# Two transformer blocks in one kernel: phase borders worked in column halves, a five-slab weight ring with the low parts in place, and loops written out

## The chip, the cores and the metric

The kernel runs on one core of a Trainium2 chip. A core has a matrix engine (TensorE, PE in the profile; its weight loads are PEld), a vector engine (VectorE, DVE), an activation engine (ScalarE, ACT), GpSimd (POOL) and a queue engine (SyncE, SP) that here issues most of the transfers. All work from SBUF, the on-chip memory of 128 partitions; PE writes to PSUM. The metric is the device time of one execution in microseconds, as the median of several.

## The reference

A 256 x 1024 activation goes through four layers' worth of sublayers in fp32. Cut to what matters:

```
h = x
h += gating_mixer(rms_norm(h)); h += relu(rms_norm(h) @ w_up[0])**2 @ w_down[0]          # "gate_in/gate_out", "mlp0"
h += dilated_attention(rms_norm(h)); h += relu(rms_norm(h) @ w_up[1])**2 @ w_down[1]     # "qkv/attn/attn_out", "mlp1"
x = rms_norm(h) * final_norm_g                                                            # "final1"
for i in range(2):
    shift, scale, gate = (silu(c) @ ada_w[i] + ada_b[i]) split in three for each of 3 sublayers
    x += 0.5 * gate0 * swiglu(rms_norm(x) * (1 + scale0) + shift0, ffn_w_in, ffn_w_out)   # "ffn0", "ffn2"
    x += gate1 * (pool_mixer if i == 0 else conv_mixer)(... )                             # "pool", "conv_in/conv_out"
    x += 0.5 * gate2 * swiglu(rms_norm(x) * (1 + scale2) + shift2, ...)                   # "ffn1", "ffn3"
return rms_norm(x) * final_g
```

d_model is 1024, the hidden width of an mlp 4096, that of an ffn 2816. The weights are some 340 MB and each is used once.

## The kernel before

**Phases and slabs.** The names at the right above are the phases, run one after the other. Tokens lie in two blocks of 128 (t = 0, 1). Weights come in *slabs* of 128 x 2048 fp32 (1 MB, two transfers each): an mlp chunk has four (two of w_up, two of w_down), 8 chunks; an ffn chunk has three (two of w_in, one of w_out), 11 chunks; 245 slabs in all. A slab is used as two fp32r parts: ACT copies `raw` to `w_hi` (L512), DVE subtracts to get `w_lo` (L865). A product is then three matmuls per tile: w_hi with xT_hi, w_lo with xT_hi, w_hi with xT_lo (L1315). `xT_hi/xT_lo` hold the normed activation transposed, `hT_hi/hT_lo` the hidden one; `up_ps` and `acc` are the PSUM results of the up and down product, `tr_ps` takes transposes (L1396).

**Ring.** `raw`, `w_hi` and `w_lo` have three places each (RING). SP loads slab n when n - 3 has been split by ACT and DVE; ACT and DVE split n when PE has used n - 3. `ahead(g)` stands in ACT's and DVE's order about where PE works on slab g, and splits slab g + 3.

**Steady chunk.** PE does the up product of chunk c (48 matmuls), then the down product of chunk c - 1, then transposes chunk c's hidden tile (`mid`). ACT and DVE make `mid` from up_ps in between, and DVE also accumulates the conditioning product `ada_acc` (L930, L933) from transfers of 1 MB that ACT issues (in mlp0, mlp1, part of qkv, ffn0, ffn1).

**A border.** The order is written out by hand on each engine and joined by semaphores. PE finishes `acc` for block 0 (`acc0_ready`), then block 1 (`slab_used`). DVE (`enter`, L900) does `products(0)`: the gated product (L968, in the second model block) and the residual addition (L971), 1024 columns each; ACT squares and sums the row (L534); POOL makes 1/rms in two steps (L476, L470); DVE scales to `xn` (L880); PE transposes xn (`turn_norm`, eight transposes); ACT applies the norm's gain (L547, L549); DVE splits into xT_hi and xT_lo (L886, L887). `first_chunk` on PE turns block 0 of the *next* phase after the last matmul of the old one, does slab g for block 0, turns block 1, and does slab g + 1 for block 0, then both slabs for block 1. In `enter` one w_lo split stands ahead of block 1's xT splits and one at the end (`before`, `after`). At mlp1 to ffn0, `final1` and the ffn's own norm follow each other (L1139 between).

The long phases' middle chunks are loops on every engine (`Fori`; three chunks a body in an mlp, one in an ffn).

## Time and profile before

| | |
|---|---|
| median of 3 runs | 1605.37 us (1604.02 to 1610.68) |
| the profiled execution | 1607.08 us, its span 1605.3 us |
| PE busy | 1524.8 us, 95% |
| PE weight loads | 1254.0 us, 78% |
| DVE busy | 1038.2 us, 65% |
| ACT busy | 707.9 us, 44% |
| read from HBM | 343.96 MB, 215 GB/s over the span |
| mean granted TensorE clock | 0.981 |

Matmuls overlap in the records (one of 512 columns is shown with about 0.4 us), so a rate is read from the distance of starts. Idle time of an engine is given in brackets with what ended it.

### The profile page before, as it was taken

Reading aid. Unit: us, or ns where it says so; the run is one execution under the profiler, and the core shown is the slowest. Engines: PE = TensorE matmul, PEld = TensorE weight load, DVE = VectorE, ACT = ScalarE, POOL = GpSimd, SP = SyncE. Lnnn points to the kernel's source line nnn. Section 1 sums busy time; section 2 is a strip of 40 time slices with the busy share of each in tenths; the row PEclk is TensorE's granted clock in tenths of the full one; section 3 lists DMA queues with packets and bytes.
Section 4 is the critical chain, followed back from the end, with each engine's and each line's share of the span. In section 5 each row is a group of like instructions: output and inputs, shape, how many; then the busy total and the mean of one; then the engine's idle time right before and its main releaser. Section 6 shows DMA issues by size and latency. Waiting matters only on the chain.

```text
span 1605.3 us, 20507 instructions
## 1 busy us (share of the span) xinstructions
PE 1524.8 (95%) x7069; PEld 1254.0 (78%) x7069; DVE 1038.2 (65%) x1110; ACT 707.9 (44%) x831; POOL 22.0 (1%) x63
## 2 busy tenths in 40 slices
PE   5899999999999999799998899998999999999997
PEld 4778888788778888678887788886788878778886
DVE  4748777545548767567887778887645464764444
ACT  5345444543545454444443434444344444454442
POOL 1000000000000000000000000000000000000000
PEclk9999999999999999899999899999999999999999
DMA  8438777557508788558896279886455546445552
GB/s 260 174 126 324 270 269 274 159 173 243 175 12 295 282 287 289 188 183 309 302 311 229 85 256 318 303 313 217 144 184 188 189 140 204 143 158 185 190 190 76
DMA packets 201892, 345.83 MB, mean 215 GB/s; under 512 B 9531, under 2 KB 105027, under 8 KB 201836
## 3 DMA queue, kind: packets, MB, share of 16 engines
q1 hardware_dynamic: 161420, 267.22, 49.5%
q10 hardware_dynamic: 40416, 77.86, 13.9%
q8 instruction: 35, 0.57, 0.1%
q14 instruction: 21, 0.17, 0.0%
HBM read 343.96 MB, written 1.09 MB: 215 GB/s over the span
## 4 chain that ended last, share of the span: by engine, by line
PE 84%; DVE 8%; ACT 3%; DMA 2%; issue 2%; POOL 1%; SPq 0%; POOLq 0%; DVEq 0%; ACTq 0%
PE up_ps L1315 51%; PE acc L1315 28%; DVE w_lo L865 3%; PE tr_ps L1396 2%; DMA ada_raw<-in_ada_w 2%; PE tr_ps L1315 1%; DVE ada_acc L933 1%; ACT w_hi L512 1%; DVE res L971 1%; ACT xn L534 1%; DVE xn L968 1%; PE tr_ps L1581 1%; ACT xn L549 1%; PE tr_ps L1495 1%; POOL rstd L470 1%
## 5 line engine op out<-in xcount | busy, mean ns | idle before, releaser
L865 DVE TENSOR_TENSOR w_lo<-raw,w_hi 128x2048 fp32r<-128x2048 f32 x245 | 561.1, 2291 | 302.4 <-ACT w_hi L512 301.3
L512 ACT ACTIVATE w_hi<-raw 128x2048 fp32r<-128x2048 f32 x245 | 469.5, 1916 | 313.1 <-PE up_ps L1315 256.7
L1315 PE MATMUL up_ps<-w_hi,xT_hi 128*128 128x512 f32 x1264 | 506.0, 400 | 22.8 <-DVE xT_lo L887 16.5
L1315 PE MATMUL up_ps<-w_hi,xT_lo 128*128 128x512 f32 x1264 | 497.5, 394 | 0.0
L1315 PE MATMUL up_ps<-w_lo,xT_hi 128*128 128x512 f32 x1264 | 497.1, 393 | 0.0
L1315 PEld LDWEIGHTS up_ps<-w_hi,xT_hi 128*128 128x128 f32 x1264 | 240.4, 190 | 75.3 <-issue 16.9
L1315 PEld LDWEIGHTS up_ps<-w_hi,xT_lo 128*128 128x128 f32 x1264 | 240.1, 190 | 51.4
L1315 PEld LDWEIGHTS up_ps<-w_lo,xT_hi 128*128 128x128 f32 x1264 | 240.8, 190 | 47.6
L933 DVE SCALAR_TENSOR_TENSOR ada_acc<-ada_raw,cond,ada_acc 128x512 f32 (+1 forms) x252 | 189.3, 751 | 15.7 <-DMA ada_raw<-in_ada_w 8.0
L1315 PE MATMUL acc<-w_hi,hT_hi 128*128 128x512 f32 x624 | 194.3, 393 | 4.8 <-DVE hT_lo L876 4.8
L1315 PE MATMUL acc<-w_hi,hT_lo 128*128 128x512 f32 x624 | 193.0, 391 | 0.0
L1315 PE MATMUL acc<-w_lo,hT_hi 128*128 128x512 f32 x624 | 192.9, 391 | 0.0
L1315 PEld LDWEIGHTS acc<-w_hi,hT_hi 128*128 128x128 f32 x624 | 116.5, 188 | 30.1 <-DVE hT_lo L876 4.0
L526 ACT ACTIVATE hT_hi<-tr_ps 128x256 fp32r<-128x256 f32 (+1 forms) x122 | 47.8, 441 | 207.4 <-PE tr_ps L1396 203.6
L1315 PEld LDWEIGHTS acc<-w_lo,hT_hi 128*128 128x128 f32 x624 | 117.7, 189 | 24.6
L1315 PEld LDWEIGHTS acc<-w_hi,hT_lo 128*128 128x128 f32 x624 | 117.5, 188 | 24.5
L876 DVE TENSOR_TENSOR hT_lo<-tr_ps,hT_hi 128x256 fp32r<-128x256 f32 (+1 forms) x122 | 55.4, 494 | 75.7 <-ACT hT_hi L526 75.4
L752 ACT ACTIVATE pre<-up_ps 128x256 f32<-128x256 f32 x88 | 33.9, 385 | 134.4 <-PE up_ps L1315 134.3
L534 ACT ACTIVATE xn<-res 128x1024 f32<-128x1024 f32 x24 | 25.7, 1072 | 78.6 <-DVE res L971 70.0
L1167 DVE TENSOR_TENSOR mid<-pre,up_ps 128x256 f32<-128x256 f32 x88 | 34.9, 416 | 22.8 <-ACT pre L752 22.8
L1396 PE MATMUL tr_ps<-flip,xn 128*128 128x128 f32 x160 | 26.4, 318 | 20.1 <-DVE xn L880 15.9
L1396 PEld LDWEIGHTS tr_ps<-flip,mid 128*128 128x128 f32 x304 | 36.6, 140 | 11.2 <-issue 4.2
(121 smaller groups left out, 788.6 us busy)
## 6 DMA issues: line engine op xcount, KB each, us to landing
raw<-in_ffn_w_in SPq DMA_DIRECT2D x176, 512.0 KB, 4.7
ada_raw<-in_ada_w ACTq DMA_DIRECT2D x72, 1024.0 KB, 6.9
raw<-in_ffn_w_out SPq DMA_DIRECT2D x88, 512.0 KB, 4.4
raw<-in_w_up SPq DMA_DIRECT2D x64, 512.0 KB, 4.7
raw<-in_w_down SPq DMA_DIRECT2D x64, 512.0 KB, 4.6
raw<-in_b_w_qkv SPq DMA_DIRECT2D x36, 512.0 KB, 4.4
raw<-in_conv_w_in SPq DMA_DIRECT2D x24, 512.0 KB, 4.6
raw<-in_a_w_in SPq DMA_DIRECT2D x16, 512.0 KB, 6.3
```

Source lines behind the costliest of these rows:

```text
L470: nc.gpsimd.tensor_tensor(dst, src, neg_half[:, 0:1], ALU.pow).then_inc(ready, 1)
L512: nc.scalar.activation(w_hi[:, slot, :], raw[:, slot, :], ACT.Copy).then_inc(hi_ready, 1)
L526: nc.scalar.activation(dst, src, ACT.Copy).then_inc(tr_hi, 1)
L534: nc.scalar.activation(xn[:, t, :], res[:, t, :], ACT.Square, accum_out=sumsq[:, t:t + 1]).then_inc(sumsq_ready[t], 1)
L549: a = nc.scalar.activation(dst, src, ACT.Identity, bias=bias, scale=scale)
L752: nc.scalar.activation(pre[:, t, 0:HALF], up_ps[:, t, 0:HALF], ACT.Silu).then_inc(silu_done, 1)
L865: nc.vector.tensor_tensor(w_lo[:, slot, :], raw[:, slot, :], w_hi[:, slot, :].bitcast(F32), ALU.subtract).then_inc(lo_ready, 1)
L876: nc.vector.tensor_tensor(lo, src, hi.bitcast(F32), ALU.subtract).then_inc(tr_read, 1)
L933: a = nc.vector.scalar_tensor_tensor(out=dst, in0=src, scalar=cond[:, k:k + 1], in1=dst, op0=ALU.mult, op1=ALU.add)
L1167: nc.vector.tensor_tensor(mid[:, t, 0:HALF], pre[:, t, 0:HALF], up_ps[:, t, HALF:UPN], ALU.mult).then_inc(ffn_mid, 1)
L1315: return nc.tensor.matmul(dst, a, b, start=start, stop=stop, skip_group_check=True)
L1396: last = nc.tensor.transpose(dst[:, q * P:(q + 1) * P], tile, ident)
```

## The change

- The ring has five places. `w_lo` is placed at the address of `raw`: DVE writes the low part over the slab it came from. SP may therefore load slab n only when PE has used slab n - 5; ACT and DVE no longer wait for PE themselves. `ahead(g)` splits slab g + 4.
- At the end of a phase PE makes `acc` in column halves of 512 (`down_halves`), each with a signal of its own (`acc_ready`), and the transposes of the next phase's block 0 stand between the two halves of block 1 (not at mlp1 to ffn0, where they stand behind, nor at the pool).
- Products, additions, squares and the scaling of a border are done in halves; the two partial sums are added by POOL's first step. xT is split in pairs of 128-column tiles, each waited for by PE. Block 1's transposes come two k-tiles later in PE's order. DVE's order in `enter` is another.
- The tails of mlp and ffn are reordered: the transposes of the last hidden chunk come earlier. In an ffn's last chunk DVE makes `mid` ahead of its w_lo split.
- The output is stored in four pieces. All `Fori` loops are written out. Some small tiles lie elsewhere (`o_tok` in xT_hi, `bias_t` in hT).

```diff
...
-RING = 3
+RING = 5
+LEAD = RING - 1
...
+        raw_at = -(-nc.sbuf_base // 32) * 32
         raw = sb("raw", [P, RING, SLAB])
+        w_lo = nc.alloc_sbuf_tensor_at("w_lo", [P, RING, SLAB], F32R, offset=raw_at)
...
             def load(g, src, view):
...
+                slot = g % RING
+                if g >= RING:
+                    sp.wait_ge(slab_used, g - RING + 1)
...
+            def split_hi(n):
+                if n < N_SLABS:
+                    slot = n % RING
                     act.wait_ge(raw_landed[slot], 32 * (n // RING + 1))
...
+                    nc.scalar.activation(w_hi[:, slot, :], raw[:, slot, :], ACT.Copy).then_inc(hi_ready, 1)
+            def ahead(g):
+                split_hi(g + LEAD)
...
+            def squares(n, t):
+                for c in range(2):
+                    if n:
+                        act.wait_ge(res_ready[t], 2 * n + c - 1)
...
+                    cols = slice(c * COLS, (c + 1) * COLS)
+                    nc.scalar.activation(xn[:, t, cols], res[:, t, cols], ACT.Square, scale=D ** -0.5,
+                                         accum_out=sumsq[:, t, c:c + 1]).then_inc(sumsq_ready[t], 1)
...
             def scale_tokens(n, t):
                 dve.wait_ge(rstd_ready[t], n + 1)
-                nc.vector.tensor_scalar(xn[:, t, :], res[:, t, :], rstd[:, t:t + 1], None, ALU.mult)\
-                    .then_inc(xn_ready, 1)
...
+                for c in range(2):
+                    cols = slice(c * COLS, (c + 1) * COLS)
+                    nc.vector.tensor_scalar(xn[:, t, cols], res[:, t, cols], rstd[:, t:t + 1], None, ALU.mult)\
+                        .then_inc(xn_ready, 1)
...
+            def norm_split(name, t, ks=range(0, KT, 2)):
+                for k in ks:
+                    fill = (KT // FILL) * t + k // FILL
+                    if k % FILL == 0:
+                        dve.wait_ge(y_half, NORM_FILLS * XT[name] + fill + 1)
+                    else:
+                        dve.wait_ge(tr_read, at[name].tr + fill + 1)
...
+                    own(nc.vector.tensor_copy(hi, src))
+                    nc.vector.tensor_tensor(lo, src, hi.bitcast(F32), ALU.subtract).then_inc(xT_ready, 1)
...
             def enter(name, products, before=(), after=(), last_norm=None):
-                products(0)
+                for c in range(2):
+                    products(0, c)
+                for g in before:
+                    ahead(g)
                 if last_norm is not None:
                     last_norm(0)
+                    for c in range(2):
+                        products(1, c)
                 scale_tokens(NORM[name], 0)
-                products(1)
+                if last_norm is None:
+                    products(1, 0)
                 if name in XT:
-                    norm_split(name, 0)
-                if last_norm is not None:
+                    norm_split(name, 0, (0, 2))
+                if last_norm is None:
+                    products(1, 1)
+                else:
                     last_norm(1)
+                if name in XT:
+                    norm_split(name, 0, (4, 6))
                 scale_tokens(NORM[name], 1)
-                for g in before:
-                    ahead(g)
                 if name in XT:
                     norm_split(name, 1)
                 for g in after:
                     ahead(g)
...
+                def products(t, c):
+                    if sub is not None and (t, c) == (0, 0):
                         dve.wait_ge(gate_ready, sub + 1)
-                    if t == 0:
-                        dve.wait_ge(acc0_ready, product + 1)
+                    if (t, c) == (TT - 1, 1):
+                        dve.wait_ge(slab_used, g + 1)
                     else:
-                        dve.wait_ge(slab_used, g + 1)
-                    src = acc[:, t, :]
+                        dve.wait_ge(acc_ready, 3 * product + 2 * t + c + 1)
+                    cols = slice(c * COLS, (c + 1) * COLS)
+                    src = acc[:, t, cols]
                     if gate is not None:
-                        own(nc.vector.scalar_tensor_tensor(out=xn[:, t, :], in0=src, scalar=gate,
-                                                           in1=gate_B[:, sub % 3, :], op0=ALU.mult, op1=ALU.mult))
-                        src = xn[:, t, :]
-                    nc.vector.tensor_tensor(res[:, t, :], res[:, t, :], src, ALU.add).then_inc(res_ready[t], 1)
+                        own(nc.vector.scalar_tensor_tensor(out=xn[:, t, cols], in0=src, scalar=gate,
+                                                           in1=gate_B[:, sub % 3, cols], op0=ALU.mult, op1=ALU.mult))
+                        src = xn[:, t, cols]
+                    nc.vector.tensor_tensor(res[:, t, cols], res[:, t, cols], src, ALU.add).then_inc(res_ready[t], 1)
...
+                def step(c, g):
                     if c == 1:
                         for m in MODS.get(name, ())[:1]:
                             modulation(name, m)
-                    ahead(g, i, 3)
+                    at_end = c == FFN_CHUNKS - 1
+                    if not at_end:
+                        ahead(g)
                     if unit0 is not None and c >= 2:
-                        ada(unit0 + c - 2, 0, i, 1)
-                    gated_mid(c, i)
-                    ahead(g + 1, i, 3)
+                        ada(unit0 + c - 2, 0)
+                    for t in range(TT):
+                        gated_mid(c, t)
+                    ahead(g if at_end else g + 1)
                     if c == 1:
                         for m in MODS.get(name, ())[1:]:
                             modulation(name, m)
...
+                    if at_end:
+                        transposed(c, 2)
+                        return
+                    transposed(c)
                     if unit0 is not None and c >= 2:
-                        ada(unit0 + c - 2, 1, i, 1)
...
+                        ada(unit0 + c - 2, 1)
+                    ahead(g + 2)
...
-            enter("pool", residual(last("pool"), 4, 0.5, 0), [last("pool") - 1])
+            enter("pool", residual(last("pool"), 4, 0.5, 0), [last("pool") - 2, last("pool") - 1])
...
-            enter("ffn2", residual(last("ffn2"), 6, 0.5, 2), [last("ffn2") - 1], [last("ffn2")])
+            enter("ffn2", residual(last("ffn2"), 6, 0.5, 2), [last("ffn2") - 2], [last("ffn2") - 1, last("ffn2")])
...
+                for q in qs:
                     k = s * UPK + q
+                    if x0 is not None and k % 2 == 0:
+                        pe.wait_ge(xT_ready, x0 + KT // 2 * t + k // 2 + 1)
...
+            def down_halves(g, t, hi, lo, k0, between=None):
+                for c in range(2):
+                    if c and between is not None:
+                        between()
+                    last = down_tile(g, t, hi, lo, k0, False, (c,), True)
+                    if (t, c) != (TT - 1, 1):
+                        last.then_inc(acc_ready, 1)
+                return last
...
+            def down_last(g, hi, lo, k0, start, ready=None, between=None):
+                for t in range(TT):
+                    if ready is not None:
+                        pe.wait_ge(tr_read, ready[0] + (t + 1) * ready[1])
                     if t == 0:
-                        last.then_inc(acc0_ready, 1)
...
+                        pe.wait_ge(lo_ready, g + 1)
+                    last = down_tile(g, t, hi, lo, k0, start)
+                    if t == 1:
+                        last.then_inc(slab_used, 1)
+                    else:
+                        pe.wait_ge(lo_ready, g + 2)
+                    last = down_halves(g + 1, t, hi, lo, k0 + 2, between if t else None)
+                last.then_inc(slab_used, 1)
...
             def turn_norm(name, t):
-                pe.wait_ge(xn_ready, 2 * XN[name] + t + 1)
-                if t == 0:
-                    pe.wait_ge(tr_read, at[name].tr)
                 for b in range(KT // FILL):
+                    pe.wait_ge(xn_ready, 4 * XN[name] + 2 * t + b + 1)
+                    if (t, b) == (0, 0):
+                        pe.wait_ge(tr_read, at[name].tr)
                     turn(xn, t, b * FILL, FILL, at[name].tr + (KT // FILL) * t + b)
...
+            def first_chunk(name, turned=True):
                 g = at[name].slab
...
+                x0 = TT * KT // 2 * XT[name]
+                if not turned:
+                    turn_norm(name, 0)
+                pe.wait_ge(lo_ready, g + 1)
+                up_tile(g, 0, 0, x0=x0)
+                pe.wait_ge(lo_ready, g + 2)
+                up_tile(g + 1, 1, 0, range(0, 2), x0)
+                turn_norm(name, 1)
+                up_tile(g + 1, 1, 0, range(2, UPK), x0).then_inc(up0_ready, 1)
+                up_tile(g, 0, 1, x0=x0).then_inc(slab_used, 1)
+                up_tile(g + 1, 1, 1, x0=x0).then_inc(slab_used, 1)
...
+                c = MLP_CHUNKS - 1
+                gb = g + 4 * c - 2
+                up_chunk(gb, (relu_done, 2 * (m0 + c - 1) + 1))
+                down_slab(gb + 2, hT_hi, hT_lo, 0, False, (mid_fill(p, name, c - 1), 1))
+                pe.wait_ge(lo_ready, gb + 4)
+                down_tile(gb + 3, 0, hT_hi, hT_lo, 2, False)
+                turn_mid(c, 0)
+                down_tile(gb + 3, 1, hT_hi, hT_lo, 2, False).then_inc(slab_used, 1)
+                turn_mid(c, 1)
+                down_last(gb + 4, hT_hi, hT_lo, 0, False, (mid_fill(p, name, c), 1),
+                          (lambda: turn_norm(after, 0)) if early else None)
+                if not early:
+                    turn_norm(after, 0)
...
                 c = FFN_CHUNKS - 1
                 gb = g + 3 * c - 1
-                up_chunk(gb, free=(ffn_mid, 2 * (f0 + c - 1) + 1, 0))
+                up_chunk(gb, (ffn_mid, 2 * (f0 + c - 1) + 1))
                 ready = mid_fill(p, name, c - 1)
+                turn_mid(c, 0)
                 pe.wait_ge(lo_ready, gb + 3)
-                pe.wait_ge(tr_read, ready + 2)
-                down_tile(gb + 2, 0, hT_hi, hT_lo, 0, False, False)
-                turn_mid(c)
-                down_tile(gb + 2, 1, hT_hi, hT_lo, 0, False, False, [0])
+                down_tile(gb + 2, 0, hT_hi, hT_lo, 0, False)
+                turn_mid(c, 1)
                 pe.wait_ge(lo_ready, gb + 4)
                 pe.wait_ge(tr_read, ready + 3)
-                down_tile(gb + 3, 0, hT_hi, hT_lo, 2, False, True).then_inc(acc0_ready, 1)
-                down_tile(gb + 2, 1, hT_hi, hT_lo, 0, False, False, [1]).then_inc(slab_used, 1)
+                down_halves(gb + 3, 0, hT_hi, hT_lo, 2)
+                down_tile(gb + 2, 1, hT_hi, hT_lo, 0, False).then_inc(slab_used, 1)
                 pe.wait_ge(tr_read, ready + 4)
-                down_tile(gb + 3, 1, hT_hi, hT_lo, 2, False, True).then_inc(slab_used, 1)
...
+                down_halves(gb + 3, 1, hT_hi, hT_lo, 2,
+                            (lambda: turn_norm(after, 0)) if after in XT else None).then_inc(slab_used, 1)
...
```

DVE at the border ffn1 to ffn2, before, from the last silu product on (L865 w_lo split, L880 scaling, L886 and L887 the split of xn):

```order
L1167 TENSOR_TENSOR mid<-pre,up_ps 128x256 [waits silu_done] x2
L865 TENSOR_TENSOR w_lo<-raw,w_hi 128x2048 [waits slab_used,hi_ready]
L876 TENSOR_TENSOR hT_lo<-tr_ps,hT_hi 128x2x128 [waits tr_hi] x2
L968 SCALAR_TENSOR_TENSOR xn<-acc,region 128x1024 [waits acc0_ready,gate_ready]
L971 TENSOR_TENSOR res<-res,xn 128x1024 [waits dve_step]
L880 TENSOR_SCALAR xn<-res,rstd 128x1024 [waits rstd_ready0]
L968 SCALAR_TENSOR_TENSOR xn<-acc,region 128x1024 [waits slab_used]
L971 TENSOR_TENSOR res<-res,xn 128x1024 [waits dve_step]
L886 CAST xT_hi<-xn 128x2x128 [waits y_half]
L887 TENSOR_TENSOR xT_lo<-xn,xT_hi 128x2x128 [waits dve_step]
L886 CAST xT_hi<-xn 128x2x128 [waits tr_read]
```

After (L831 w_lo split, L847 scaling, L940 and L943 product and addition, L860 and L861 the split of xn):

```order
L940 SCALAR_TENSOR_TENSOR xn<-acc,region 128x512 [waits acc_ready,gate_ready]
L943 TENSOR_TENSOR res<-res,xn 128x512 [waits dve_step]
L940 SCALAR_TENSOR_TENSOR xn<-acc,region 128x512 [waits acc_ready]
L943 TENSOR_TENSOR res<-res,xn 128x512 [waits dve_step]
L831 TENSOR_TENSOR w_lo<-raw,w_hi 128x2048 [waits hi_ready]
L847 TENSOR_SCALAR xn<-res,rstd 128x512 [waits rstd_ready0]
L847 TENSOR_SCALAR xn<-res,rstd 128x512
L940 SCALAR_TENSOR_TENSOR xn<-acc,region 128x512 [waits acc_ready]
L943 TENSOR_TENSOR res<-res,xn 128x512 [waits dve_step]
L860 CAST xT_hi<-xn 128x2x128 [waits y_half]
L861 TENSOR_TENSOR xT_lo<-xn,xT_hi 128x2x128 [waits dve_step]
L860 CAST xT_hi<-xn 128x2x128 [waits tr_read]
```

The 1024-column steps have become pairs of 512, the w_lo split stands ahead of the scaling, and block 1's first half is added ahead of the first xT pair.

PE at the border gate_out to mlp0, before: the last three matmul pairs of block 1, the transposes of xn, the first matmuls of mlp0.

```order
L1315 MATMUL acc<-w_hi,xT_hi 128x512 x2
L1315 MATMUL acc<-w_lo,xT_hi 128x512 x2
L1315 MATMUL acc<-w_hi,xT_lo 128x512 x2
L1396 MATMUL tr_ps<-flip,xn 128x128 [waits tr_read,xn_ready]
L1396 MATMUL tr_ps<-flip,xn 128x128 x3
L1396 MATMUL tr_ps<-flip,xn 128x128 [waits tr_read]
L1396 MATMUL tr_ps<-flip,xn 128x128 x3
L1315 MATMUL up_ps<-w_hi,xT_hi 128x512 [waits xT_ready,lo_ready]
L1315 MATMUL up_ps<-w_lo,xT_hi 128x512
L1315 MATMUL up_ps<-w_hi,xT_lo 128x512
```

After, from the same place, with the transposes between the halves of block 1:

```order
L1284 MATMUL acc<-w_hi,xT_hi 128x512
L1284 MATMUL acc<-w_lo,xT_hi 128x512
L1284 MATMUL acc<-w_hi,xT_lo 128x512
L1376 MATMUL tr_ps<-flip,xn 128x128 [waits tr_read,xn_ready]
L1376 MATMUL tr_ps<-flip,xn 128x128 x3
L1376 MATMUL tr_ps<-flip,xn 128x128 [waits tr_read,xn_ready]
L1376 MATMUL tr_ps<-flip,xn 128x128 x3
L1284 MATMUL acc<-w_hi,xT_hi 128x512
L1284 MATMUL acc<-w_lo,xT_hi 128x512
L1284 MATMUL acc<-w_hi,xT_lo 128x512
L1284 MATMUL acc<-w_hi,xT_hi 128x512
L1284 MATMUL acc<-w_lo,xT_hi 128x512
```

Six matmuls into acc now stand behind the transposes of xn and ahead of the first up product.

## Rows read from the trace of the kernel before

**Rows 1.** Stretches: us; PE, PEld, DVE, ACT, POOL busy; granted clock, DMA share, GB/s.

```profile
800.00:840.00 40.00, 40.00 (x183) 33.11 (x182) 32.75 (x37) 16.41 (x18) 0.00 (x0) 1.00 0.90 307
```

**Rows 2.** Timeline of PE, mlp0: start, duration, operation; transposes that end chunks.

```profile
189.20 1.03 PE L1396 MATMUL tr_ps<-flip,mid 128*128 128x128 f32 x8
...
211.85 1.04 PE L1396 MATMUL tr_ps<-flip,mid 128*128 128x128 f32 x8
...
234.53 1.03 PE L1396 MATMUL tr_ps<-flip,mid 128*128 128x128 f32 x8
```

**Rows 3.** Waits of PE: total us, times, longest us.

```profile
PE up_ps L1315 <- DVE xT_lo L887: 16.5, 9, 4.1
PE tr_ps L1396 <- DVE xn L880: 15.9, 10, 3.6
...
PE acc L1315 <- DVE hT_lo L876: 4.8, 6, 1.9
```

**Rows 4.** Timeline of PE, ffn1 to ffn2; in brackets idle before and releaser.

```profile
1090.17 0.70 PE L1315 MATMUL acc<-w_hi,hT_hi 128*128 128x512 f32 x2 [0.48 <-DVE hT_lo L876]
...
1098.69 1.09 PE L1396 MATMUL tr_ps<-flip,xn 128*128 128x128 f32 x8 [1.45 <-DVE xn L880]
...
1101.84 0.76 PE L1315 MATMUL up_ps<-w_hi,xT_hi 128*128 128x512 f32 x1 [2.06 <-DVE xT_lo L887]
...
1107.33 0.50 PE L1315 MATMUL up_ps<-w_hi,xT_hi 128*128 128x512 f32 x1 [0.24 <-DVE w_lo L865]
```

**Rows 5.** Timeline of DVE and ACT, same border, chain of block 0.

```profile
1093.27 1.23 DVE L968 SCALAR_TENSOR_TENSOR xn<-acc,region 128x1024 f32<-128x1024 f32 x1 [2.92 <-PE acc L1315]
...
1094.53 1.23 DVE L971 TENSOR_TENSOR res<-res,xn 128x1024 f32<-128x1024 f32 x1
...
1095.79 1.06 ACT L534 ACTIVATE xn<-res 128x1024 f32<-128x1024 f32 x1 [7.01 <-DVE res L971]
...
1097.88 0.75 DVE L880 TENSOR_SCALAR xn<-res,rstd 128x1024 f32<-128x1024 f32 x1 [2.13 <-POOL rstd L470]
```

**Rows 6.** Groups by form, DVE and ACT: busy us, mean ns, then idle.

```profile
L865 DVE TENSOR_TENSOR w_lo<-raw,w_hi 128x2048 fp32r<-128x2048 f32 x245 | 561.1, 2291 | 302.4 <-ACT w_hi L512 301.3 <-DVE region L1247 0.9
...
L876 DVE TENSOR_TENSOR hT_lo<-tr_ps,hT_hi 128x512 fp32r<-128x512 f32 x34 | 22.0, 686 | 16.9 <-ACT hT_hi L526 16.9
...
L930 DVE TENSOR_SCALAR ada_acc<-ada_raw,cond 128x512 f32 x28 | 13.5, 481 | 0.0
...
L512 ACT ACTIVATE w_hi<-raw 128x2048 fp32r<-128x2048 f32 x245 | 469.5, 1916 | 313.1 <-PE up_ps L1315 256.7 <-PE acc L1315 51.7 <-DMA raw<-in_a_w_in 2.9
...
L628 ACT ACTIVATE pre<-up_ps 128x512 f32<-128x512 f32 x32 | 19.2, 599 | 35.1 <-PE up_ps L1315 35.1
```

**Rows 7.** Timeline of PE, mlp0 to qkv.

```profile
295.14 0.47 PE L1315 MATMUL up_ps<-w_hi,xT_hi 128*128 128x512 f32 x1 [1.19 <-DVE xT_lo L887]
...
298.51 1.09 PE L1396 MATMUL tr_ps<-flip,xn 128*128 128x128 f32 x8 [0.37 <-DVE xn L880]
...
300.71 0.50 PE L1315 MATMUL up_ps<-w_hi,xT_hi 128*128 128x512 f32 x1 [1.11 <-DVE w_lo L865]
```

**Rows 8.** Timeline of PE, mlp1 to ffn0.

```profile
654.06 1.08 PE L1315 MATMUL acc<-w_hi,hT_hi 128*128 128x512 f32 x2 [1.86 <-DVE hT_lo L876]
...
669.09 1.09 PE L1396 MATMUL tr_ps<-flip,xn 128*128 128x128 f32 x8 [2.23 <-DVE xn L880]
...
671.58 0.77 PE L1315 MATMUL up_ps<-w_hi,xT_hi 128*128 128x512 f32 x1 [1.40 <-DVE xT_lo L887]
...
679.01 1.33 PE L1396 MATMUL tr_ps<-flip,xn 128*128 128x128 f32 x5 [2.97 <-DVE xn L880]
```

**Rows 9.** Timeline of PE, the pool's first matmuls.

```profile
881.04 8.15 PE L1315 MATMUL tr_ps<-region,xn 128*128 128x128 f32 x48 [4.05 <-DVE xn L880]
```

**Rows 10.** Timeline of PE, second chunk of gate_in.

```profile
33.46 0.47 PE L1315 MATMUL up_ps<-w_hi,xT_hi 128*128 128x512 f32 x1 [1.35 <-ACT region L606]
```

**Rows 11.** Loads of raw issued inside ffn0: us from issue to landing.

```profile
DMA to landing us min/median/max: 3.9/5.7/7.6
```

594 lines of the change are left out of this document (243 added, 351 removed).

## Prediction

> **What bounds the kernel now.** I read the page's busy times first: TensorE (PE) is busy 95% of the span. Then the table by stretches: inside the big layers PE is busy all of 40 us, at the full granted clock, even where the DMA share is 0.90 [rows 1]. The timeline of PE gives the rate there: an mlp0 chunk of 96 matmuls of 512 columns and 8 transposes takes 22.65 us [rows 2]; with 0.8 for the transposes that is 0.228 us a matmul, and 5.5 us for a slab of 24. So the layers themselves give nothing. What is left is what PE waits for: about 80 us, and the longest entries in the list of waits are the norm's split output xT_lo (16.5 us in 9 waits), the norm's scaled output xn (15.9 us in 10) and hT_lo (4.8 us) [rows 3]. All of them lie at the border between one phase and the next.
>
> **One border, read closely (ffn1 to ffn2).** PE waits 0.48 us for hT_lo, 1.45 for xn, 2.06 for xT_lo, and then runs at the lower clock: from 1101.84 to 1107.33 us lie 12 matmuls and 8 transposes, nominally 12 x 0.228 + 0.6 = 3.3 us, and the waits inside are 0.24, so 1.9 us go to the clock; the first matmul takes 0.76 us against 0.50 in the later row, so the granted clock has fallen to its 1.2 GHz level after 3.5 us of waits [rows 4]. The sum is 4.2 us of waits and 1.9 of clock. The chain that PE waits for is serial: gated product 1.23, addition 1.23, square 1.06 (and about 0.2 to read its sum), two steps on GpSimd (they lie in the 2.13 us that DVE waits for rstd), scaling 0.75 [rows 5].
>
> **The change at such a border.** PE finishes token block 0 of acc by column halves. Call T0 the end of its second half. Before, 18 or 24 matmuls stand behind T0 ahead of the transposes (4.1 or 5.5 us); now always 18 (4.1 us), then transposes, then 6 matmuls (1.4 us) that cover the split of xn. Price of the pieces on DVE: 512-column operations with two inputs 0.69, scaling 0.48; on ACT 0.60 [rows 6], plus 0.2 for the sum. The gated pair I take as 0.75 + 0.69, a little over the nearest row. The first half is accumulated 1.4 us before T0, so its products run until T0 + 0.3, those of the second until T0 + 1.7; square T0 + 2.55, GpSimd T0 + 3.5. Here the changed DVE order has one w_lo split (2.29 [rows 6]) ahead of the scaling, which therefore ends its first half at T0 + 4.5: PE arrives at 4.1 and waits 0.4. First xT pair: DVE does the products of block 1's first half until 6.35, then the pair until 7.1; PE has its transposes and the 6 matmuls until 7.0, wait 0.2. The next pairs come at 7.8, 9.95 and 10.7 and PE needs them at 8.5, 9.9 and later; block 1's xn is there at 11.4 when PE comes at 11.3. The wait for hT_lo stays at about 0.5, since one w_lo split still stands ahead of it on DVE. Sum of waits about 1.25 instead of 4.2, no single one long, so I take the clock as staying up. Worth 3.0 + 1.9 = **5 us**, and the same at ffn2 to conv_in: **10 us** for the two.
>
> *What a rule makes of the pieces.* The row shows that a 1024-column operation takes 1.22 to 1.23 and a 512-column one 0.69, so each extra instruction costs 0.15 us [rows 5, 6]. The Trainium skill (Perfetto Trace Analysis, Optimizing Scalar/DVE Operations) gives an access overhead of some 60 ns on SBUF and 125 ns on PSUM for a DVE instruction; by that the two halves would be about 0.1 us cheaper per pair and each gated border 0.2 us better. The measured rows decide.
>
> **Ungated borders.** gate_out to mlp0, mlp0 to qkv, attn_out to mlp1 have the same shape without the gate and with no w_lo split inside the border (slabs are now split four ahead, so g+1 is ready: that was the 1.11 us in [rows 7]). There the scaled half is ready at T0 + 3.1, before PE's 4.1, and the first pair at about 6.2 to 6.6 against PE's 6.5: waits of 0 to 0.2. Their waits before are 1.19 + 0.37 + 1.11 = 2.7 [rows 7], and at mlp0 to qkv about 1 more for hT_lo (the rest of the six in [rows 3]). Worth 2.7, 3.6 and 2.7. conv_out to ffn3 is gated without a split and had 2.1 + 0.2 + 1.1: worth 3.3. Together **12 us**.
>
> **mlp1 to ffn0**, with two norms in a row, lies otherwise: 1.86 + 2.23 + 1.40 + 2.97 us of waits, and a lower clock after them [rows 8]. New chain for block 0: products T0 + 0.95, first norm T0 + 2.7, its two output halves 4.2, second square 5.0, GpSimd 5.9, then block 1's products, which are queued in front, 6.4, scaling 6.9; PE has nothing left at T0 + 5.5 and waits 1.4, then 1.1 for the first pair. The third pair is queued on DVE behind block 1's last norm (rstd at T0 + 12.9, two halves until 14.4): a wait of some 3.3 us where PE had none. Block 1's xn follows at 16.6 instead of 17.7, with 30 matmuls behind it where there were 36 (1.4 us). That is 2.5 us, or up to 3.8 if the clock is up. The hT_lo wait shrinks from 1.86 to about 0.8 by the split tail, and with it goes the low clock behind it (the first pair takes 1.08 us there and 0.70 in [rows 4]), 1.6 us by estimate from the 1.9 above. Taken: **5.5 us** (3 to 8).
>
> **The pool phase gives nothing back.** PE waits 4.05 us for xn there [rows 9] and needs both blocks whole. The changed DVE order has two w_lo splits (4.6 us) between block 0's products and its scaling, which at their end (T0 + 6.7) come 3 us behind rstd; the last tail ends its block 0 about 1 us earlier, the pieces cost 0.6. I get the start of the pool 1.2 us later and ffn1's border behind it 0.8 us better: **-0.4** (-2 to +2).
>
> **Start.** ACT now does four w_hi splits and the fifth ahead of the first gelu, one more than before, 1.92 us [rows 6], and PE transposes block 1 six matmuls later. PE already waits 1.35 us for that gelu [rows 10]; I work out 2.8: **-1.4** (-2 to 0).
>
> **End.** After the last matmul the last half has 0.75 + 0.69 in place of 1.23 + 1.23, square 0.8 in place of 1.25, but two output pieces in place of one: **+1.2**.
>
> **Loops written out: 0.** The transposes that end mlp0's chunks lie 22.65 us apart inside the old loop body of three and 22.68 across its branch [rows 2], so a branch costs PE 0.03 us at most; 40 such ends are 1 us. The Trainium skill (Runtime: NRT & Kernel Launch, Instruction fetch mechanics) says that a taken branch to code outside the resident pages must wait for a fetch, which would make written-out code faster; the interval does not agree, and the page alone has no price for it.
>
> **Loads: the cost that the change adds.** SP's load of slab n waited for the splits of n-3; now it waits until PE has used n-5 (the low part sits in raw's place). Behind it are queued later loads, ACT's w_hi split of n, and behind that ACT's silu and, on DVE, w_lo, the ada sums and mid. In ffn0 and ffn1, the tightest stages, a load lands 5.7 us (3.9 to 7.6) after issue [rows 11]. Released at a chunk's start and landed at +6.2, it gives w_hi at 8.1, w_lo at 10.4, ada until 13.2, mid at 14.0; PE asks for mid at 16.4 of its 16.8 us. So 2.4 us are spare, and 1 at the 7.6 us landing. Bounds: 0 by that, and at a landing of 11 us, which no row there has, 2.4 us per chunk. I take 0.
>
> **Sum:** 10 + 12.3 + 5.5 - 0.4 - 1.4 + 1.2 = 27 us. The profiled execution took 1607.1 (span 1605.3); the median of the three runs is 1605.4. 1605.4 - 27 = **1578**.
>
> **Rivals.** (a) Half the gain: DVE's own queue gives the time back, because the products of block 1 and the splits stand ahead of the xT pairs, and every piece that is 0.2 us dearer than taken shifts PE at eight borders. If waits of 1.5 us stay at each and the clock falls at the two gated ones, 6 x 1.2 + 4 = 11 to 14 us are lost: 1591. For it: the spare times above are a few tenths. (b) The other side: the later loads. Place: ffn0 and ffn1, 16 chunks with two ada loads each. It starts at landings over 8.6 us and makes the kernel slower than before by 0.5% where they reach 6.2 + 2.4 + (27 + 8)/16 = 10.8 us; at 11.5 it is 1605 - 27 + 46 = 1624. Against it: loads now come one by one instead of in bursts, and the longest there is 7.6 [rows 11]. (c) More than taken: clock up also through mlp1 to ffn0 and the pool, whose lower clock the stretch after them shows, and no start penalty: 27 + 9 = 36 us, 1569. (d) The change doesn't shorten the chain: signals for halves are there, but DVE is still held by an earlier entry of its queue (the w_lo split that needs a late w_hi), so xn comes when it came before: 1602 to 1608.
>
> **How the numbers follow.** Forecast (1573 to 1584) 0.52; (a) 0.22, (c) 0.12, (b) 0.07, (d) 0.07. The range that leaves out (b) and (d) and most of the tail of (a): 1567 to 1593. A run of this kernel can tell about 0.5%, 8 us: faster than 1597 0.87, within 0.05, slower 0.08.
>
> **What would show it.** Right: PE's waits for xT_lo and xn fall from 32 to under 12 us; the granted clock has no dip at ffn1 to ffn2 and ffn2 to conv_in but has one at mlp1 to ffn0 and the pool; PE's steady chunks stay 16.8 us; the wait for the first gelu grows to 2.8. Wrong: idle PE inside ffn0 or ffn1 chunks that ends with mid or w_lo (b), or waits of over 1 us for xT_lo at the gated borders (a).

## Result and profile after: 1596.6 us, a ratio of 0.9948

The changed kernel takes 1596.6 us (median of 5, 1594.7 to 1601.7) where the kernel before takes 1605.4; the ratio is 0.9948, 95% interval 0.9927 to 0.9969. Faster, as forecast, but by 9 us and not by 27, so the time lies above the range (1567 to 1593). Here and below, a ratio is taken between executions of both kernels in one session, and can differ by some 0.002 from the quotient of the two medians. The page of after, with the engines' busy time, the chain that ended last, and the group of ScalarE's (ACT's) splits:

```profile
span 1594.8 us, 17438 instructions
PE 1523.5 (96%) x7069; PEld 1249.8 (78%) x7069; DVE 1047.8 (66%) x1220; ACT 713.4 (45%) x879; POOL 32.9 (2%) x63
...
PE 80%; DVE 9%; DMA 4%; ACT 3%; issue 1%; POOL 1%; SPq 0%; DVEq 0%; POOLq 0%; ACTq 0%
...
L498 ACT ACTIVATE w_hi<-raw 128x2048 fp32r<-128x2048 f32 x245 | 469.1, 1918 | 287.8 <-DMA raw<-in_ffn_w_in 132.3
```

The last row is the first hint: the split of a slab now waits for its DMA. In the kernel before the same group waited for PE. The groups by line, first of before and then of after, show who ended the idle time ahead of the splits:

```profile
L512 ACT ACTIVATE w_hi<-raw 128x2048 fp32r<-128x2048 f32 x245 | 469.5, 1916 | 313.1 <-PE up_ps L1315 256.7 <-PE acc L1315 51.7 <-DMA raw<-in_a_w_in 2.9
...
L498 ACT ACTIVATE w_hi<-raw 128x2048 fp32r<-128x2048 f32 x245 | 469.1, 1918 | 287.8 <-DMA raw<-in_ffn_w_in 132.3 <-DMA raw<-in_w_up 42.0 <-DMA raw<-in_w_down 31.0
```

PE's waits of after (waited for: us in total, times, longest), against [rows 3]:

```profile
PE tr_ps L1376 <- DVE xn L847: 9.7, 6, 3.3
PE up_ps L1284 <- DVE xT_lo L861: 7.4, 4, 3.8
...
PE acc L1284 <- DVE hT_lo L841: 5.7, 5, 3.7
...
PE tr_ps L1465 <- DVE mod_sum L915: 4.0, 3, 2.5
PE acc L1284 <- ACT region L676: 3.9, 1, 3.9
PE up_ps L1284 <- DVE mid L1138: 3.6, 3, 1.2
```

The border waits have halved (xT_lo and xn from 32.4 to 17.1 us). In their place stand waits that the prediction did not have: 3.9 us of attention's first matmul for ACT's copies (0.8 in the kernel before), 4.0 for `mod_sum`, the sums of the conditioning that PE's next transposes need (1.7 before), 3.6 for mid, and one of 3.7 for hT_lo.

**Where the time went, step by step.** I took the start of each first matmul of a chunk from PE's timeline of both kernels and subtracted. Gains are positive:

```
stage                               predicted   measured
start and gate_in                     -1.4        -2.4
gate_out to mlp0                      +2.7        +3.0
mlp0 to qkv                           +3.6        +3.6
qkv's last chunk and attention         0          -5.3
attn_out to mlp1                      +2.7        +3.4
mlp1, second chunk                     0          -4.2
mlp1 to ffn0                          +5.5        +2.1
pool and its borders                  -0.4        +1.0
ffn1, second and third chunk           0          -2.1
ffn1 to ffn2                          +5          +2.6
ffn2 to conv_in                       +5          +4.6
conv_out to ffn3                      +3.3        +2.3
end                                   +1.2        +1.5
steady chunks and the rest             0          +0.4
sum                                   +27         +10.5 (spans 1605.3, 1594.8)
```

So the six plain borders brought 19.5 of the 22.3 us that were summed for them, and 11.6 us went in three stages where the prediction had written 0; 3.4 more went at mlp1 to ffn0. Two of the places, read closely.

**Attention.** ACT in after (start, duration, [idle before <- what ended it]); L676 are the copies out of qkv's last chunks that PE waits for:

```profile
389.24 1.92 ACT L498 ACTIVATE w_hi<-raw 128x2048 fp32r<-128x2048 f32 x1 [5.24 <-DMA raw<-in_b_w_out]
391.06 0.58 ACT L676 ACTIVATE region<-up_ps 128x512 f32<-128x512 f32 x1
...
398.55 1.92 ACT L498 ACTIVATE w_hi<-raw 128x2048 fp32r<-128x2048 f32 x1 [5.48 <-DMA raw<-in_b_w_out]
404.17 1.91 ACT L498 ACTIVATE w_hi<-raw 128x2048 fp32r<-128x2048 f32 x1 [3.70 <-DMA raw<-in_w_up]
405.99 1.06 ACT L676 ACTIVATE region<-up_ps 128x512 f32<-128x512 f32 x2
```

and what SyncE issued (start, duration of the issue), with PE's matmul behind:

```profile
382.52 1.36 SPq L302 DMA_DIRECT2D bias_t<-bias_rows  x2
387.03 0.83 SPq L331 DMA_DIRECT2D raw<-in_b_w_out  x2
```

```profile
407.20 1.12 PE L1284 MATMUL acc<-region 64*128 64x128 f32 x7 [3.88 <-ACT region L676]
```

The second slab of attn_out is asked for at 387.03 and its split starts at 398.55: 11.5 us. The next one comes late too, and both copies, whose sums PE had finished at about 401 and 403, stand behind its split. PE's first score matmul comes 14.9 us after the start of qkv's last chunk and not 11.8. So 3.1 of attention's 5.3 us are this wait; the other 2.2 are lost behind it, where PE's granted clock is lower (the rows are with a_move below).

**mlp1 to ffn0.** ACT, then PE:

```profile
652.64 1.91 ACT L498 ACTIVATE w_hi<-raw 128x2048 fp32r<-128x2048 f32 x1 [5.64 <-DMA raw<-in_ffn_w_in]
654.46 1.07 ACT L508 ACTIVATE hT_hi<-tr_ps 128x512 fp32r<-128x512 f32 x2
```

```profile
657.54 0.80 PE L1284 MATMUL acc<-w_hi,hT_hi 128*128 128x512 f32 x1 [3.74 <-DVE hT_lo L841]
```

The first hT tile was in PSUM from 650.6; ACT held it for 3.9 us behind a slab of the next phase. So 1.86 us of [rows 8] became 3.74, and the gain of the split border behind it (waits of 1.18, 1.40 and 1.17 us, where 1.4, 1.1 and 3.3 had been worked out) was eaten.

### The profile page after: what moved, and what is told of

Its sections match the earlier page's. It is cut to its first block, busy times and chain, and to the rows that moved or that the text cites. A ratio compares the mean times of both kernels' runs of the same rounds, so it can differ in the third digit from the quotient of the medians.

```text
span 1594.8 us, 17438 instructions
## 1 busy us (share of the span) xinstructions
PE 1523.5 (96%) x7069; PEld 1249.8 (78%) x7069; DVE 1047.8 (66%) x1220; ACT 713.4 (45%) x879; POOL 32.9 (2%) x63
## 4 chain that ended last, share of the span: by engine, by line
PE 80%; DVE 9%; DMA 4%; ACT 3%; issue 1%; POOL 1%; SPq 0%; DVEq 0%; POOLq 0%; ACTq 0%
PE up_ps L1284 48%; PE acc L1284 27%; PE tr_ps L1376 3%; DVE w_lo L831 3%; DMA raw<-in_ffn_w_in 2%; ACT w_hi L498 2%; PE tr_ps L1284 1%; DVE ada_acc L904 1%; DMA raw<-in_w_down 1%; DVE res L943 1%; DVE xn L940 1%; DMA raw<-in_w_up 1%; PE tr_ps L1558 1%; ACT xn L518 1%; DVE xT_lo L861 1%
## 5 line engine op out<-in xcount | busy, mean ns | idle before, releaser
L831 DVE TENSOR_TENSOR w_lo<-raw,w_hi 128x2048 fp32r<-128x2048 f32 x245 | 559.3, 2289 | 289.9 <-ACT w_hi L498 289.7
L1284 PE MATMUL acc<-w_hi,hT_hi 128*128 128x512 f32 x624 | 199.9, 394 | 5.7 <-DVE hT_lo L841 5.7
L1284 PE MATMUL acc<-w_hi,hT_lo 128*128 128x512 f32 x624 | 197.9, 391 | 0.0
L1284 PE MATMUL acc<-w_lo,hT_hi 128*128 128x512 f32 x624 | 197.7, 391 | 0.0
L904 DVE SCALAR_TENSOR_TENSOR ada_acc<-ada_raw,cond,ada_acc 128x512 f32<-128x512 f32 x252 | 189.1, 751 | 12.8 <-DMA ada_raw<-in_ada_w 5.1
L841 DVE TENSOR_TENSOR hT_lo<-tr_ps,hT_hi 128x256 fp32r<-128x256 f32 (+1 forms) x122 | 55.7, 492 | 46.0 <-ACT hT_hi L508 45.5
L518 ACT ACTIVATE xn<-res 128x512 f32<-128x512 f32 x48 | 30.6, 638 | 56.7 <-DVE res L943 48.6
L1376 PE MATMUL tr_ps<-flip,mid 128*128 128x128 f32 x304 | 44.5, 273 | 2.7 <-DVE mid L1138 1.4
```

Of the source, the lines that this page charges most:

```text
L518: nc.scalar.activation(xn[:, t, cols], res[:, t, cols], ACT.Square, scale=D ** -0.5, accum_out=sumsq[:, t, c:c + 1]).then_inc(sumsq_ready[ ...
L831: nc.vector.tensor_tensor(w_lo[:, slot, :], raw[:, slot, :], w_hi[:, slot, :].bitcast(F32), ALU.subtract).then_inc(lo_ready, 1)
L841: nc.vector.tensor_tensor(lo, src, hi.bitcast(F32), ALU.subtract).then_inc(tr_read, 1)
L904: a = nc.vector.scalar_tensor_tensor(out=dst, in0=src, scalar=cond[:, k:k + 1], in1=dst, op0=ALU.mult, op1=ALU.add)
L1284: return nc.tensor.matmul(dst, a, b, start=start, stop=stop, skip_group_check=True)
L1376: last = nc.tensor.transpose(dst[:, q * P:(q + 1) * P], tile, ident)
```

## The experiments

**Theory L (late loads).** In the kernel before, the load of slab n is released by the splits of n-3, and its own split stands three slabs of PE time later in ACT's order. In the changed kernel it is released when PE has used n-5 and its split stands four slabs ahead of use: one slab, 5.5 us, lies between. A load with company takes longer, and everything behind the split in ACT's order waits. **Theory D (order)**: ACT and DVE now split four slabs ahead (a *lead* of four), which puts one more low part (2.29 us) ahead of urgent work on VectorE (DVE). **Rival R**: the halves bring less than summed, the ring costs nothing.

### Parts alone: b_flat, b_ring5, a_ring3, a_lead3

b_flat is the kernel before with its loops written out:

```
-                with pe.Fori(0, MLP_BODIES) as i:
-                    for b in range(MLP_BODY):
-                        step(2 + b, False, i, MLP_BODY)
+                for c in range(2, MLP_CHUNKS):
+                    step(c, False)
```

> The kernel before with its loops written out and nothing else: same instructions, same order, same ring of three. All theories: no effect of its own, 1605.4 +/- 1.5 us. If it is off by more than 3 us, part of the missing gain belongs to the written-out loops (the larger program), not to the ring.

Measured: ratio 0.999 (0.9978 to 1.0003), 1606.6 us. Written-out loops do nothing, as predicted. A trace is of one execution, and b_flat's shows how far to trust a single stage: with the same work in the same order as before, it is 0.9 us shorter at mlp1 to ffn0, 1.2 at the pool and its borders, and 0.5 longer in attention.

b_ring5 adds the ring to b_flat, the borders stay whole:

```
-RING = 3
+RING = 5
+LEAD = RING - 1
...
-                        sp.wait_ge(hi_ready, n - RING + 1)
-                        sp.wait_ge(lo_ready, n - RING + 1)
+                        sp.wait_ge(slab_used, n - RING + 1)
...
-                n = g + RING
+                n = g + LEAD
```

> The kernel before (borders whole, tails in the old order, loops written out) with only the ring changed: five slabs, low parts in place, a load released by the use of the slab five before, splits four slabs ahead. Theory L (late loads: a load now starts only when PE has used slab n-5, and its split stands in ScalarE's order one slab's use later, about 5.6 us, while landings with company take 4 to 10 us; the late split holds what stands behind it): the ring alone costs what the phases of the changed kernel show against the kernel before away from the borders, 3.9 (attention) + 4.2 (mlp1, second chunk) + 2.6 (gate_in) + 2.1 (ffn1) = 12.8 us and something at the borders: 1618 us, 1612 to 1624. Rival R (the borders in halves simply bring less than summed, the ring is free): 1605 +/- 2.

Measured: 1622.1 us, ratio 1.0085 (1.0063 to 1.0107). The ring alone costs 14 us; its trace has the loss at attention (8.1 us), in mlp1's second chunk (2.7), in and ahead of ffn1 (5.3) and at ffn1 to ffn2 (2.6), and 5 to 6 us of gain at the other borders, where the second slab is ready earlier. R falls, at least for the ring.

a_ring3 is the changed kernel with the old ring, a_lead3 the changed kernel with `LEAD = RING - 2`. Both need the low part of a phase's second slab placed by hand in DVE's order at seven borders:

```
                 scale_tokens(NORM[name], 1)
+                for g in second:      # last(name) - 1
+                    ahead(g)
                 if name in XT:
                     norm_split(name, 1)
```

> The changed kernel with the ring of before (three slabs, low parts in a buffer of their own, a load released by the split of the slab three before), borders in halves, reordered tails and written-out loops kept. Theory L: the 18 us that are missing come back for the most part: 1580 us, 1577 to 1586; before attention PE no longer waits 3.9 us, mlp1's second chunk takes 26.6 us and not 30.8. Rival R: the halves bring only what was measured, 1596 +/- 3.

> The changed kernel with its ring of five in place, but each slab split three slabs ahead of its use instead of four, so that one slab's use more (about 5.6 us) lies between the release of a load and its split. Theory L: most of the waits <-DMA raw of ScalarE and the waits behind them go: 1585 us, 1579 to 1589. Rival R: 1596 +/- 3. Rival C (the loads are late for lack of DMA throughput, not for their late start): little changes either, 1593 to 1598, and a_ring3 likewise stays high.

Measured: 1621.0 us (1.0072, 1.0050 to 1.0093) and 1620.1 us (1.0068, 1.0048 to 1.0089). Both missed, by 41 and 35 us, but not for the reason that was asked after. The stages in question did as L says: mlp1's second chunk took 27.0 us in a_ring3 and 25.8 in a_lead3 (30.8 in after), ffn1's chunks lost nothing, and from mlp1's last chunk to ffn0's first matmul a_lead3 needed 4.8 us less than the kernel before. But PE had a new wait (a_ring3):

```profile
PE up_ps L1288 <- DVE w_lo L834: 29.5, 7, 7.2
```

Seven waits, one for each border: with halves, PE arrives at the second slab before DVE has scaled the second block and come to its low part. In this placement it takes the lead of four to have the second slab ready in time.

### The second slab earlier, and late splits moved away: a_ring3b, a_lead3b, a_move, a_lead3bm

a_ring3b and a_lead3b move the two added lines above `scale_tokens`.

> a_ring3 with one instruction of VectorE moved at seven borders: the low part of a phase's second slab is made before the second tile is scaled, not behind it. In a_ring3 PE stood 29.5 us in seven waits for that low part. Theory L with this placement as the reason that a_ring3 came out slow: the seven waits go and the borders return to the changed kernel's own steps (first chunks 2 us shorter than before, where a_ring3 has them 3.1 to 4.7 longer), 38 us less than a_ring3: 1583 us where the kernel before is 1608, 1578 to 1590, so under the changed kernel. Rival P (the old ring can't give the second slab early, since its split waits for PE's use of the last slabs of the phase ahead): the waits move but stay, 1600 to 1615.

> a_lead3 with the same instruction moved. Theory L: 1582 us where the kernel before is 1608, 1577 to 1589: attention starts without the 3.9 us wait of the changed kernel, mlp1's second chunk takes 26 and not 30.8 us, mlp1 to ffn0 gets its 5 us. Rival P: the waits for the second slab's low part stay at half or more, 1600 to 1612.

Measured: 1599.3 us (0.9950, 0.9933 to 0.9968) and 1597.3 us (0.9940, 0.9920 to 0.9959), 16 and 15 us over what was expected. Some 22 us came back of the 38; the wait is still there (a_ring3b):

```profile
PE up_ps L1288 <- DVE w_lo L834: 16.5, 7, 4.0
```

So rival P was half right. The halves with the old ring give 0.9950, with the new ring 0.9948: the same total from different places. The changed kernel buys the second slab in time at seven borders, and pays for it in attention, mlp1, gate_in and ffn1.

a_move leaves ring and lead alone and only moves splits behind urgent copies (the same on DVE); three of its places:

```
                 hidden(0, 1, g)
-                ahead(g + 1)
                 transposed(0)
+                ahead(g + 1)
...
                     ahead(g + 1)
+                    if c == MLP_CHUNKS - 1:
+                        transposed(c)
                     ahead(g + 2)
-                    transposed(c)
+                    if c < MLP_CHUNKS - 1:
+                        transposed(c)
...
-                if u == 1:
-                    ahead(at["attn"].slab - 1)
+                if u in (1, 4):
+                    ahead(at["attn"].slab - (2 if u == 1 else 1))
```

> The changed kernel, ring of five and lead of four as they are; only the order on ScalarE and VectorE changes at four places, so that no split of a late slab stands ahead of work that PE waits for: in qkv's last chunk and in attention (one split moved behind the copies), and in both mlps' first and last chunk (one split moved behind the copies of the turned hidden values). Theory L (the harm is done by what stands behind a late split, in order): 3.9 us at attention, 4.2 in mlp1's second chunk, 3.4 of mlp1 to ffn0 come back, 1587 us, 1583 to 1592, and nothing changes in the ffns. Rival S (PE itself waits for late slabs and would wait for them anyway): 1596 +/- 2.

Measured: 1592.5 us (0.9908, 0.9890 to 0.9925), 4 us under the changed kernel by the medians and 6 by the ratios (1587 was expected). By stages: mlp1 to ffn0 got its 3.7 us back, as expected. In mlp1's second chunk only 0.7 of 4.2 came back: the order of ACT's splits is not the reason there. In attention PE's first score came at 11.8 us again, the 3.1 us of waiting were gone, and yet the stage ended only 0.2 us earlier, because what followed ran at a lower granted clock. Stretches of 10 us (busy PE, PEld, DVE, ACT, POOL, then the granted clock, DMA share, GB/s), first before, then after, then a_move, then b_ring5_ada4 of further down:

```profile
405.00:415.00 10.00, 7.28 (x34) 5.63 (x32) 7.77 (x10) 5.28 (x8) 0.00 (x0) 0.85 0.74 248
415.00:425.00 10.00, 9.95 (x57) 8.23 (x56) 5.37 (x13) 5.44 (x13) 0.00 (x0) 0.81 0.69 220
```

```profile
405.00:415.00 10.00, 6.82 (x25) 4.86 (x26) 6.90 (x11) 7.56 (x11) 0.00 (x0) 0.66 0.39 140
415.00:425.00 10.00, 10.00 (x49) 8.39 (x49) 3.95 (x10) 3.45 (x10) 0.00 (x0) 0.66 0.12 40
```

```profile
405.00:415.00 10.00, 7.98 (x30) 6.07 (x29) 6.05 (x12) 5.37 (x10) 0.00 (x0) 0.63 0.40 141
415.00:425.00 10.00, 10.00 (x40) 8.46 (x39) 2.25 (x8) 4.47 (x8) 0.00 (x0) 0.52 0.13 39
```

```profile
405.00:415.00 10.00, 7.15 (x36) 5.65 (x37) 4.75 (x9) 6.92 (x12) 0.00 (x0) 0.87 0.47 144
415.00:425.00 10.00, 10.00 (x56) 8.36 (x56) 3.29 (x11) 3.25 (x8) 0.00 (x0) 0.78 0.14 41
```

The score and probability matmuls up to attn_out took 53.5, 55.7, 58.6 and 54.6 us in the four.

a_lead3bm is a_lead3b with these moves.

> Both: a_lead3b with the moves of a_move. Theory L: the lead of three already takes the late splits away, so the moves add little: 1579 us, 1574 to 1587, within 3 us of a_lead3b. Rival: the two add up, 10 us under a_lead3b.

Measured: 1607.2 us (0.9993, 0.9979 to 1.0006), 10 us over a_lead3b. With a lead of three a split can't be moved back without PE feeling it: against a_lead3b, mlp0 to qkv lost 4.0 us, mlp1 to ffn0 4.8 and attention 2.2, and PE waited 4.1 us for w_lo in the down products, a wait that a_lead3b has not. A miss of mine: the moves need the slab to spare.

### Each suspected cost alone: a_dve, a_bias, a_ada4, and all moves: a_best

a_dve moves two things on DVE:

```
+                        if (c, s) == (1, 0):
+                            for sub in MODS.get(name, ()):
+                                modulation(name, sub)
                         ahead(g + s)
-                        if (c, s) == (1, 0):
-                            for sub in MODS.get(name, ()):
-                                modulation(name, sub)
...
                 for g in after:
+                    if g == after[-1] and name in FFN_AT:
+                        first_mid(name)
                     ahead(g)
```

> The changed kernel with two moves on VectorE alone; ScalarE, PE and the loads keep their order. In each ffn the first gated tile is made before the last of the two low parts that stand behind the border (they take 4.5 us in a row in the changed kernel, and PE waited 1.2, 1.2 and 1.2 us for the tile), and in mlp1's second chunk the modulation's sums are read before the low part of a slab that PE needs a chunk later (PE waited 2.5 us for them). Theory D (a lead of four puts one more low part of 2.29 us ahead of what PE waits for on VectorE at the start of a phase): 1.2 us less at ffn1, ffn2 and ffn3 each and 2 us less in mlp1's second chunk: 5 us, 1592 us where the kernel before is 1607. Theory L alone (only late loads matter): 1597 +/- 1.5.

Measured: 1593.4 us (0.9921, 0.9893 to 0.9949). The medians alone would not part this from the changed kernel, but the steps do: mlp1's second chunk loses 0.9 us and not 4.2, the first chunks of ffn0, ffn2 and ffn3 are 1.35, 1.3 and 1.35 us shorter (ffn1's is not), and the trace's last matmul comes 5.2 us earlier. DVE and PE around the modulation in after:

```profile
497.15 3.10 DVE L904 SCALAR_TENSOR_TENSOR ada_acc<-ada_raw,cond,ada_acc 128x512 f32<-128x512 f32 x4
500.17 2.28 DVE L831 TENSOR_TENSOR w_lo<-raw,w_hi 128x2048 fp32r<-128x2048 f32 x1
502.37 1.28 DVE L915 TENSOR_REDUCE mod_sum<-tr_ps 128x4 f32<-128x512 f32 x2
```

```profile
503.21 1.17 PE L1465 MATMUL tr_ps<-flip,ada_acc 128*128 128x128 f32 x6 [2.49 <-DVE mod_sum L915]
```

and PE in a_dve:

```profile
501.64 1.16 PE L1471 MATMUL tr_ps<-flip,ada_acc 128*128 128x128 f32 x8 [0.29 <-DVE mod_sum L922]
```

PE came there earlier than in the kernel before, since its border was shorter, and found DVE with a low part for a later chunk in hand. The same at the ffns (ffn2 in after):

```profile
1108.60 4.48 DVE L831 TENSOR_TENSOR w_lo<-raw,w_hi 128x2048 fp32r<-128x2048 f32 x2
1113.01 0.41 DVE L1138 TENSOR_TENSOR mid<-pre,up_ps 128x256 f32<-128x256 f32 x1
```

```profile
1113.56 0.47 PE L1284 MATMUL up_ps<-w_hi,xT_hi 128*128 128x512 f32 x1 [1.19 <-DVE mid L1138]
```

a_bias swaps SyncE's two bias loads and the load behind them:

```
+            load(g + 1, down_src(b_w_out[0], DOWNK * P), down_view)
             sp.wait_ge(xn_ready, 4 * XN["qkv"] + 4)
             for h in range(2):
                 load_bias(sp, h)
-            load(g + 1, down_src(b_w_out[0], DOWNK * P), down_view)
```

> The changed kernel with two of SyncE's DMAs swapped: the second slab of attn_out is asked for before the two bias loads of 384 KB, not behind them. In the changed kernel this slab took from 387 to 398.5 us to land beside them and an adaLN load, and ScalarE stood 5.5 us for it with the last qkv copies behind. Theory L: the slab lands 2 to 4 us earlier, and qkv's last chunk to mlp1 takes 2 to 4 us less (82.5 us in the changed kernel, 78.6 in the kernel before): 1594 us where the kernel before is 1607. If the bias loads then become late themselves, attention's first logits wait instead, and nothing is won.

Measured: 1597.8 us (0.9942, 0.9923 to 0.9961), no gain. ACT in a_bias:

```profile
393.98 1.92 ACT L498 ACTIVATE w_hi<-raw 128x2048 fp32r<-128x2048 f32 x1 [1.61 <-DMA raw<-in_b_w_out]
402.84 1.91 ACT L498 ACTIVATE w_hi<-raw 128x2048 fp32r<-128x2048 f32 x1 [6.94 <-DMA raw<-in_w_up]
404.65 1.06 ACT L676 ACTIVATE region<-up_ps 128x512 f32<-128x512 f32 x2
```

The slab came 4.6 us earlier, but the next one only 1.3 (its split starts at 402.84 and not 404.17), and the copies stand behind that one. PE's first score came 0.6 us earlier, and the matmuls behind it took 1.3 us longer. Moving one load ahead of another helped the last of them little here, where the DMA engines were full (the last section has the rows).

a_ada4 takes company away: from the second unit of the adaLN weights on, it loads only a quarter of the columns. It leaves out the rest, so the conditioning of the later layers is not the reference's; no instruction is dropped. It reads 289 MB where the changed kernel reads 344.

```
-                act.dma_start(up_view(ada_raw[:, s, :]), up_src(ada_w_2[u // ADA_UNITS], s, col))\
+                n = UPN if u == 0 else UPN // 4
+                act.dma_start(up_view(ada_raw[:, s, :])[:, :, 0:n], up_src(ada_w_2[u // ADA_UNITS], s, col)[:, :, 0:n])\
```

> The changed kernel with the loads of the adaLN weights cut to a quarter of their columns from the second unit on (so the modulations of the later layers are not the reference's; all instructions stay). This takes 58 of the 346 MB off the DMA engines, and most company off the slab loads of mlp0, qkv, mlp1, ffn0 and ffn1. Theory L: splits come on time at attention, mlp1 to ffn0 and in ffn1: 3.5, 3 and 2 us less than the changed kernel, 1588 us where the kernel before is 1607; ffn2, conv and ffn3 do not change. Theory S (a load simply starts too late, company or not; 5.6 us after its release its split is due): 1595 to 1597.

Measured: 1585.9 us (0.9866, 0.9840 to 0.9892), 11 us under the changed kernel by the medians and 13 by the ratios. In the stages of the table above, attention lost 1.7 us against the kernel before and not 5.3 (its wait of 3.1 is gone, what is left lies behind it), mlp1 to ffn0 gained 6.3 (predicted 5.5), gate_out to mlp0 and mlp0 to qkv 3.5 and 4.6; ffn1's second and third chunk still lose 1.4 of 2.1. ffn2, conv_in and ffn3, which have no adaLN loads, are the same to within 0.5 us. Theory S falls as it stands: the late start needs the company to do harm. The issues of attn_out's slabs (KB each, median us to landing), after and then a_ada4:

```profile
raw<-in_b_w_out SPq DMA_DIRECT2D x4, 512.0 KB, 8.4
```

```profile
raw<-in_b_w_out SPq DMA_DIRECT2D x4, 512.0 KB, 5.8
```

a_best is a_move, a_dve and a_bias together, with one more split moved from qkv into attention and

```
             for c in range(4):
-                ahead(g)
+                if c:
+                    ahead(g)
...
+                if c == 0:
+                    ahead(g)
                 ahead(g + 1)
```

on ACT in gate_in.

> The changed kernel with all moves together: those of a_move, a_dve and a_bias, one more split of qkv moved into attention, and gate_in's first gelus before the fifth slab's split. If the losses were these four (splits of late slabs ahead of urgent copies, one low part too many ahead of urgent work on VectorE, a slab behind the bias loads, gelus behind three splits), their steps add: 4 (a_move) + 5 (a_dve) + 3 (attention) + 2.5 (gate_in with its clock) = 14.5 us under the changed kernel, 1583 us where the kernel before is 1607 (0.985), range 1579 to 1589. If they overlap, 1590.

Measured: 1584.4 us (1576.5 to 1588.3), ratio 0.9841 (0.9812 to 0.9869): faster than both kernels, 12 us under the changed one by the medians and 17 by the ratios. The sum is near the expected 1583, but the trace, which is of its slowest execution (1588.3), does not have the gains all where I had put them: 1.4 us at the first gelus, yes, but 1.6 more lost in the next two chunks; of attention's 5.3 us, 4.1 are still lost; in ffn2's second chunk PE waits 2.4 us for mod_sum, and that with a granted clock of 0.78 to 0.88 around it costs 3.6 (a_dve waits 1.5 us there and loses 0.7, the changed kernel waits 0.6 and loses nothing).

### The control: b_ada4 and b_ring5_ada4

The edit is that of a_ada4, made in b_flat and in b_ring5.

> The kernel before with loops written out (b_flat) and the adaLN loads cut to a quarter as in a_ada4 (so later modulations are not the reference's). Control for a_ada4, which came out 14 us under the changed kernel. Theory L (in the ring of five the split is due 5.6 us after the load's release, so company on the DMA engines reaches PE; in the ring of three three slabs' time lies between): nearly nothing, 1603 to 1607 us where the kernel before is 1606. Rival (the adaLN loads cost any version 10 us and more, by DMA or otherwise): 1590 to 1596.

> b_ring5 with the same quarter loads. The ring alone cost 14 us (1622 where before is 1608). Theory L: most of that was company: it costs 2 to 6 us over b_ada4, 1606 to 1611. Rival (the ring costs by its order alone, one more low part ahead on VectorE): the 14 us stay, 1618 to 1622.

Measured: 1605.0 us (0.9988, 0.9973 to 1.0003), as expected, and 1603.7 us (0.9973, 0.9957 to 0.9989), under the 1606 to 1611 that theory L had. With the earlier runs:

```
ratio to the kernel before       all adaLN loads    a quarter of them
borders whole, ring of three         0.999               0.9988
borders whole, ring of five          1.0085              0.9973
borders halved, ring of three        0.9950                -
borders halved, ring of five         0.9948              0.9866
```

This settles the sum: less company does nothing for the ring of three, and takes the cost of the ring of five away as a whole (what is left is 0.0015 below b_ada4, with intervals that overlap). Subtracting the stages of the traces tells where. Of the 14.4 us that the quarter loads save the ring of five beyond what they save b_flat, 7.5 lie in attention (2.6 of PE's wait, 4.8 behind it at a lower clock), 2.7 at mlp1 to ffn0, 2.6 ahead of the pool and 1.7 at ffn1 to ffn2. That part goes with late landings, which take a late release and company together. More time cures attention as fewer bytes do: with a lead of three and all loads (a_lead3b) it loses 1.7 us, as in a_ada4. Rival C, DMA time alone, falls with that. The adaLN loads don't do it by their own lateness: DVE's waits for ada_raw are 8.1 us in b_flat and 5.6 in b_ring5.

The quarter loads do not touch the rest of the ring's cost, 8 us in all, and most of it is where D puts it: PE still waits for what DVE brings late (mod_sum 2.3 us in mlp1's second chunk and 1.3 in ffn1's, hT_lo 1.3 ahead of the pool), and in b_ring5_ada4 mlp1's second chunk loses 2.7 us against b_ada4, ffn1's second and third chunk 1.8, the stretch ahead of the pool 1.6, the end 1.0. That the sum comes out near nothing is because earlier second slabs bring 7 us at the borders. And the halves, with loads out of the way, are worth 0.9866 / 0.9973 = 0.989, 17 us (with a ring of three the halves were not run with the quarter loads).

ACT's splits in b_ring5_ada4, by line:

```profile
L511 ACT ACTIVATE w_hi<-raw 128x2048 fp32r<-128x2048 f32 x245 | 468.9, 1917 | 255.8 <-DMA raw<-in_ffn_w_in 129.0 <-DMA raw<-in_w_up 34.0 <-DMA raw<-in_w_down 31.3
```

They still wait for DMAs nearly as long as in after. So this wait alone is no sign of a loss. It costs where it is longer than the spare time of what stands behind it.

## The prediction, point by point

- **What bounds the kernel, steady chunks, loops.** Right: chunks stayed at 22.65 and 16.8 us, b_flat showed the loops to be free. By the Trainium skill (Runtime: NRT & Kernel Launch, Instruction fetch mechanics) the written-out code could have been faster, without branches to pages not resident; b_flat's interval (0.9978 to 1.0003) shows no such gain. The list of PE's waits before has two entries above hT_lo's 4.8 us that the prediction's list leaves out: 7.6 us for a DMA at the start, and this one for the second slabs of the borders, which it prices further down (the 1.11 us of [rows 7]) and which most of these experiments turn on:

```profile
PE up_ps L1315 <- DVE w_lo L865: 4.9, 6, 1.1
```

- **Ungated borders, 12.3 us summed.** Measured 3.0, 3.6, 3.4 and 2.3. The waits behind it went as said: at gate_out to mlp0 PE has none left. The last one is 1 us short for a wait for mid that the sum had not; without it (a_dve) it gives 3.7.
- **Gated borders, 5 each.** ffn2 to conv_in 4.6, right. ffn1 to ffn2 2.6. The clock stayed up as said (0.83 in the ten us from 1100 before, 1.00 after), and the waits were 0.37 us for hT_lo and 1.01 for xn, none for xT_lo (0.5, 0.4 and 0.2 worked out). But the step "the next pairs come at 7.8, 9.95 and 10.7" ended the chain too soon: behind the border DVE has two low parts and then mid, 1.2 us late. With mid first it is 3.9; the rest is the size of the term.
- **mlp1 to ffn0, 5.5.** The border's first two waits were about right; the third was 1.17 us and not 3.3, which is luck for the sum. The step that failed is "the hT_lo wait shrinks from 1.86 to about 0.8": it grew to 3.7, behind a late slab. In a_ada4 the stage gains 6.3 (in b_ada4 1.6).
- **Pool -0.4, end +1.2.** +1.0, within its bounds, but b_flat has +1.2 there without any change of order, so this stage shows nothing; and +1.5.
- **Start -1.4.** Gelu's wait became 2.4 (2.8 worked out); 1.6 us more went to the clock between 50 and 60 us, outside the bound of -2.
- **Loads: 0.** This is the step that failed: "I take 0" for the cost that the ring adds. Alone it costs 14 us (b_ring5), and in the changed kernel 11.6 us went in three stages and 3.4 at mlp1 to ffn0. The release rule was described rightly, and so was the queue behind it. Then the price was worked out in steady chunks of ffn0 and ffn1, with a landing of 5.7 us, and only there: a place with 2.4 us to spare, where indeed nothing was lost. But the landings that hurt lie where other DMAs cluster (bias tables and adaLN beside attn_out: 11.5 us), and the urgent work behind the split lies where phases start and end. "Loads now come one by one instead of in bursts" does not hold there. This is shown for the wait at attention (3.1 us) and for mlp1 to ffn0 (a_move gets 3.7 back).
- **A term that the sum lacks.** The lead of four puts one more low part ahead of mod_sum and mid in DVE's order, and the prediction prices that at neither. It is most of mlp1's second chunk (3.3 of 4.2 us come back in a_dve) and the 1.2 us of waiting at the start of ffn0, ffn2 and ffn3. In ffn1's second and third chunk it fits too (a wait of 0.9 us for mod_sum; 2.1 us lost, 1.4 with a quarter of the adaLN loads, 0.1 with a lead of three), but no run moved that instruction alone.
- **Rivals.** (b) had the mechanism, but its place was wrong and so its chance of 0.07 and its all-or-nothing size. (a) had a near size (1591) from another cause. The waits for xT_lo and xn, told to fall below 12 us, are at 17.

What stays open: why the granted clock in attention is 0.85 and 0.81 before, 0.66 in the changed kernel and down to 0.52 in a_move, where no long wait precedes it. It does not go with the ring of five as such: b_ring5_ada4 has 0.87 and 0.78. From the first score to attn_out the kernels take 53.5 to 58.9 us, so 2.2 of attention's 5.3 us, and the 4.8 us behind the wait in b_ring5, have no shown cause. Nor is it shown why the first chunks of gate_in lose 1.6 us to the clock. No run here holds the clock fixed.

## To carry to other kernels

Depth of a ring is two numbers: how many slabs ahead of use the split stands, and how much time lies between a load's release and its split. A change can raise the first and cut the second; write both down, and price the second at the stretch where most other DMAs run, not in the steady loop. In an in-order queue, put what the bound engine waits for ahead of preparation for later, and do so at every start and end of a phase. To tell a lack of DMA time from a bad order, cut the bytes of an unrelated load, run the same cut on the kernel before, and compare by stages: a cost of 8 us and a gain of 7 hid here in a difference near nothing.

## What the runs showed of the hardware

Between 388 and 404 us the DMA engines were busy in all 40 slices and moved 370 GB/s:

```profile
DMA  9999999999999999999999999999999999999999
GB/s 384 374 323 333 312 307 333 338 312 348 392 407 374 292 200 300 405 428 379 440 374 374 399 410 415 404 410 394 379 389 389 384 384 389 394 374 389 389 384 389
DMA packets 3174, 5.92 MB, mean 370 GB/s; under 512 B 174, under 2 KB 942, under 8 KB 3173
```

Single slices of 0.4 us reach 440. The Trainium skill (DMA: Bandwidth & Descriptors, Where 436 GB/s comes from) says that the fabric's ceiling is 435 GB/s and that a load from HBM is bound by some 358 per core; the ceiling agrees with the slices to within 5, the bound, which that passage gives without a condition, does not agree with a mean of 370 over 16 us, with only this one core at work. In this stretch a slab's two loads of 512 KB took 11.5 us to its split, against medians to landing of 4.3 to 5.4 us for most slabs. I had not expected that two tables of 384 KB and two to three adaLN loads of 1 MB would double a landing, nor that of 4.6 us won by swapping two loads (a_bias) only 1.3 would reach the next. The granted clock was the other surprise: in a_move 3.1 us of waits ahead of attention are gone and the matmuls behind take 2.9 us longer, at 0.63 and 0.52 where the changed kernel has 0.66. That the one makes the other is not shown: a_ada4 and b_ring5_ada4 have no such wait either, and take 0.5 and 1.2 us less there than the changed kernel.
